# Input, memory, gains and convolution taps handed over as columns in a three-layer transformer kernel

## Chip, cores and metric

The kernel runs on one core of one Trainium2 chip. The metric is the device time of one execution in microseconds (us); lower is better.

## What is computed

One sequence of 256 positions, width 1024, goes through two layers of one kind and one of another, all in fp32. Cut to what matters here:

```python
def rms_norm(x, g):
    y = x * rsqrt(mean(x * x, axis=-1, keepdims=True) + EPS)
    return y * g

for layer in range(2):
    if layer == 1: shared_kv = shared_moba_kv(h, positions, kv_norm_g, w_kv, k_norm_g)
    h = h + 0.5 * swiglu(rms_norm(h, ffn1_norm_g[layer]), ...)       # width 2816
    u = rms_norm(h, mix_norm_g[layer]) @ w_in
    primary = conformer_conv(...) if layer == 0 else moba_attention(...)
    mem_out = memory_attention(q_mem, rms_norm(mem, mem_norm_g[layer]), w_mem_kv[layer], ...)
    h = h + concat([primary, mem_out]) @ w_o[layer]
    h = h + 0.5 * swiglu(rms_norm(h, ffn2_norm_g[layer]), ...)
h = second_block(h, norm_pre, norm_post, w_in, ..., conv_qk, ...)    # attention, mLSTM
```

`conformer_conv` is a depthwise convolution of 31 taps over 768 channels with a bias, then a layer norm and silu. `mem` has 256 rows of 1024; keys and values of each layer are `rms_norm(mem, g) @ w_mem_kv`. The second block has a depthwise convolution of 4 taps (`conv_qk`).

## The kernel before

Activations are held as columns: 128 partitions by 8 chunks by 256 positions (`hT`). Each product is made in single fast passes of a split number: an operand is rounded to a high part (`xh`, `whi`, by ScalarE) and a rest (`xl`, `wlo`, by VectorE), and three of the four products are summed. The weights are cut by `weight_plan` (L126) into 403 slots of up to 128x1024 numbers (512 KB). SyncE loads slot j into one of seven raw buffers once the rest of slot j-7 is made (L2892). `use(slot)` on ScalarE and VectorE (L1297, L1900) splits the slots up to slot+4 into five buffers each, and before that runs what `side(slot)` has for this slot. TensorE takes the slots in order; a slot of a feed-forward product is four groups, each of two 512-wide products with the high weights and two 256-wide with the rests (`two_blocks`, L541). `side` (L512) puts small products between slots. So each engine's order is written out by hand, and semaphores named in `signals` (L329) tie them.

**Start (L687, L1390, L2028, L2869).** SyncE loads a row of gains, then x in two tiles of 128 rows (512 KB each), then weight slots. TensorE turns the gain row and the 16 blocks of x; ScalarE and VectorE copy them from PSUM into `hT`. ScalarE rounds `hT` times gain into `xh` (`prep`), VectorE makes `xl`, and both split the first slots. Then come the squares for the first norm: ScalarE squares the four pairs of chunks (128x512), VectorE adds them into `acc` (`squares`, L1976), and `norm_sums` (L649) sums them over the partitions by four small products at slots 3, 75, 101, 169, 237, 269 and 337 (`NORM`, L35).

**Gains (L681, L1408, L1910).** The other seven gain rows are loaded by SyncE at slot 4 into `grow`, turned by TensorE at slot 6 and copied by VectorE. `mem_gain_load` waits on ScalarE for that copy, then loads the memory's gain row to all partitions over the same buffer.

**Memory (L1410, L1416, L2004, L665).** ScalarE loads `mem` as rows at slot 5 after six small loads, squares it at slot 12, and POOL makes the rows' norm factors. VectorE multiplies rows, factor and gain (`mem_row`: slots 16, 33, 37). TensorE turns the 16 blocks of each layer in groups of eight at slots 18, 20, 36 and 40 (`turn`), and ScalarE and VectorE split them (`turned`). The products are at slots 28 (`MKV0`) and 86 (`MKV1`); ScalarE reads them out by `mem_rows` (L1552).

**Taps (L760, L2120, L2847, L2881, L1051).** SyncE loads the 31 taps, bias and layer norm rows, TensorE turns them in six products at slot 46, VectorE copies them twice, SyncE writes one copy to DRAM and reads it back by fours. The four-tap rows are turned in eight products at slot 337.

## Time and profile before

| | us |
|---|---|
| median of 3 runs | 1241.22 |
| lowest, highest | 1240.76, 1243.17 |
| profiled execution, its own time | 1241.3 |
| its span, first to last instruction | 1239.7 |
| TensorE busy in the span | 1216.3 (98%) |
| VectorE, ScalarE, POOL busy | 882.0, 681.1, 60.6 |
| TensorE's mean granted clock | 0.996 |

The page gives busy time per engine and the costliest groups of instructions. The timeline lists instructions in order of time, where x14 says that fourteen were merged; the brackets tell how long the engine stood idle before and what released it. SPq and ACTq are DMA issues of SyncE and ScalarE. PE is TensorE, DVE VectorE, ACT ScalarE.

### The profile page before, as it was taken

The numbers are of one execution on the slowest core, as the hardware profiler recorded it, in microseconds if no ns is written. First come the engines' busy times: TensorE is split into PE (matmuls) and PEld (weight loads), VectorE is DVE, ScalarE is ACT, GpSimd is POOL, SyncE is SP. The second block draws the span as 40 slices with busy tenths as digits, with TensorE's granted clock in tenths as the row PEclk, the third lists the DMA queues.
The fourth block names the chain that finished last, engine by engine and source line by source line (L and its number), as shares of the span: only waits on it lengthen the run. The fifth ranks groups of instructions, "written<-read, shape, count | busy, mean of one in ns | idle before, by whom it ended". The sixth has DMA issues, their size and how long they took to land.

```text
span 1239.7 us, 18893 instructions
## 1 busy us (share of the span) xinstructions
PE 1216.3 (98%) x7518; PEld 1066.9 (86%) x7518; DVE 882.0 (71%) x1256; ACT 681.1 (55%) x1032; POOL 60.6 (5%) x89
## 2 busy tenths in 40 slices
PE   7999999989999999999999999999999999999998
PEld 6888888967888888888888888988888899888996
DVE  6686856875787775777775677577776666666875
ACT  5655544533666554555554456656555545556463
POOL 4000100100010000000000122000000000000000
PEclk9999999989999999999999999999999999999999
DMA  8766566671466655666655556047665566556450
GB/s 273 229 206 195 169 186 199 208 185 42 154 201 189 189 177 186 196 188 187 192 179 180 162 175 191 26 128 215 186 199 173 177 189 184 169 139 181 141 171 34
DMA packets 205654, 215.46 MB, mean 174 GB/s; under 512 B 9809, under 2 KB 192593, under 8 KB 205567
## 3 DMA queue, kind: packets, MB, share of 16 engines
q1 hardware_dynamic: 202998, 210.76, 56.5%
q10 hardware_dynamic: 2568, 3.50, 0.8%
q8 instruction: 60, 0.98, 0.3%
q14 instruction: 28, 0.22, 0.1%
HBM read 212.19 MB, written 2.03 MB: 173 GB/s over the span
## 4 chain that ended last, share of the span: by engine, by line
PE 90%; DVE 4%; ACT 4%; issue 2%; DMA 0%; ACTq 0%; POOL 0%; SPq 0%
PE psum L505 88%; DVE wlo L1896 1%; ACT whi L1294 1%; PE psum L671 0%; PE psum L953 0%; DMA xn<-in_x 0%; ACT qn L1598 0%; PE psum L699 0%; DVE x L1988 0%; ACT qT L1659 0%; ACTq L1409 0%; ACT L1735 0%; DVE small L2487 0%; ACT zob L1735 0%; ACT pb L1780 0%
## 5 line engine op out<-in xcount | busy, mean ns | idle before, releaser
L505 PE MATMUL psum<-x,whi 128*128 128x512 f32 (+1 forms) x2288 | 636.2, 365 | 3.8 <-ACT whi L1294 2.4
L1896 DVE TENSOR_TENSOR wlo<-raw,whi 128x1024 fp32r<-128x1024 f32 (+2 forms) x403 | 474.1, 1189 | 184.3 <-ACT whi L1294 181.3
L1294 ACT CAST whi<-raw 128x1024 fp32r<-128x1024 f32 (+2 forms) x403 | 406.0, 1022 | 163.2 <-PE psum L505 150.6
L505 PEld LDWEIGHTS psum<-x,wlo 128*128 128x128 f32 x1960 | 370.1, 189 | 74.3 <-DVE wlo L1896 1.8
L505 PE MATMUL psum<-x,wlo 128*128 128x256 f32 x1960 | 414.5, 279 | 0.7 <-DVE wlo L1896 0.7
L505 PEld LDWEIGHTS psum<-x,whi 128*128 128x128 f32 x2288 | 351.6, 190 | 5.8 <-ACT whi L1294 2.8
L505 PE MATMUL psum<-g,whi 128*128 128x512 f32 x704 | 220.1, 394 | 0.0
L505 PEld LDWEIGHTS psum<-g,wlo 128*128 128x128 f32 x704 | 132.2, 188 | 30.5
L505 PE MATMUL psum<-whi,x 128*128 128x512 f32 (+1 forms) x512 | 141.2, 376 | 0.1
L505 PE MATMUL psum<-g,wlo 128*128 128x256 f32 x704 | 139.2, 279 | 0.0
L505 PEld LDWEIGHTS psum<-g,whi 128*128 128x128 f32 x704 | 106.5, 188 | 0.0
L505 PEld LDWEIGHTS psum<-whi,x 128*128 128x128 f32 x512 | 90.0, 190 | 16.1 <-ACT zob L1707 0.3
L505 PE MATMUL psum<-wlo,x 128*128 128x512 f32 (+1 forms) x256 | 86.7, 374 | 0.0
L1341 ACT COPY pr<-psum 128x512 f32<-128x512 f32 x44 | 25.8, 586 | 66.3 <-PE psum L505 66.2
L1341 ACT COPY gr<-psum 128x512 f32<-128x512 f32 x44 | 25.8, 586 | 60.7 <-PE psum L505 60.5
L1970 DVE TENSOR_TENSOR pr<-psum,pr 128x512 f32<-128x512 f32 x44 | 30.4, 690 | 35.5 <-ACT pr L1341 35.5
L505 PEld LDWEIGHTS psum<-wlo,x 128*128 128x128 f32 x256 | 46.3, 190 | 8.6
L1371 ACT ACTIVATE x<-hT,gcol 128x256 fp32r<-128x256 f32 x64 | 28.5, 500 | 45.5 <-DVE hT L2105 29.1
L1970 DVE TENSOR_TENSOR gr<-psum,gr 128x512 f32<-128x512 f32 x44 | 30.3, 690 | 31.3 <-ACT gr L1341 31.2
L1988 DVE SCALAR_TENSOR_TENSOR x<-hT,gcol,x 128x256 fp32r<-128x256 f32 x64 | 28.8, 497 | 18.2 <-ACT x L1371 18.2
L1430 ACT ACTIVATE gr<-gr 128x512 f32<-128x512 f32 x44 | 27.7, 633 | 21.5 <-DVE gr L2054 21.5
L1439 ACT CAST g<-pr 128x512 fp32r<-128x512 f32 x44 | 27.4, 623 | 19.3 <-DVE pr L2062 19.3
(322 smaller groups left out, 851.5 us busy)
## 6 DMA issues: line engine op xcount, KB each, us to landing
raw<-in_ffn_w_gate SPq DMA_DIRECT2D x88, 512.0 KB, 4.4
raw<-in_ffn_w_up SPq DMA_DIRECT2D x88, 512.0 KB, 4.2
raw<-in_ffn_w_down SPq DMA_DIRECT2D x80, 512.0 KB, 3.9
raw<-in_w_in SPq DMA_DIRECT2D x52, 512.0 KB, 3.8
raw<-in_w_o SPq DMA_DIRECT2D x16, 512.0 KB, 4.6
raw<-in_a_w_in SPq DMA_DIRECT2D x14, 512.0 KB, 4.7
raw<-in_w_kv SPq DMA_DIRECT2D x16, 384.0 KB, 3.1
raw<-in_w_mem_kv SPq DMA_DIRECT2D x8, 512.0 KB, 3.9
```

Source lines behind the costliest of these rows:

```text
L505: return pe.matmul(o, l, r, start=start, stop=stop, skip_group_check=True)
L1294: act.copy(held(B.whi[:, i % SPLIT, :], *n), held(B.raw[:, i % RAW, :], *n)).then_inc(*s.hi.now(i))
L1341: act.copy(out, psum[:, b:b + 2, S:2 * S]).then_inc(*s.half.now(key))
L1371: act.activation(x[:, c, :], hT[:, c, :], ACT.Copy, scale=gcol[:, c, gi:gi + 1]).then_inc(*s.x_hi.now((gen, c)))
L1430: act.activation(r, r, ACT.Silu).then_inc(*s.silu.now((f, p)))
L1439: act.copy(F.gh[:, 2 * p:2 * p + 2, :], in_pairs(F.pr[:, p % 2, :])).then_inc(*s.g_hi.now((f, p)))
L1896: dve.tensor_tensor(held(B.wlo[:, i % SPLIT, :], *n), held(B.raw[:, i % RAW, :], *n), held(B.whi[:, i % SPLIT, :], *n).bitcast(F32), ALU.s ...
L1970: dve.tensor_tensor(out, psum[:, b:b + 2, 0:S], out, ALU.add).then_inc(*s.sum.now(key))
L1988: dve.scalar_tensor_tensor(out=xl[x][:, c, :], in0=hT[:, c, :], scalar=gcol[:, c, gi:gi + 1], in1=xh[x][:, c, :].bitcast(F32), op0=ALU.mul ...
```

## The change

The host lays out six arrays besides the weights: x and mem as columns, all ten gains as columns, the convolution taps with bias and layer norm rows as columns and a second time by fours, and the four taps as columns. The turning on TensorE and the copies behind it are gone. TensorE turns the identity eleven times at the start instead, into a bank that nobody reads. x comes in three pieces of 2, 2 and 4 chunks, the last behind two weight slots, and slot 0 is split in two halves; slot 2 is split before the squares. ScalarE issues the gains' load, and applies one silu first. The memory is loaded twice, as rows for the squares and as columns; ScalarE and VectorE split column chunk c times gain at slots 14 to 22 and 36 to 44, and `mem_rows` multiplies by the row's norm factor on reading out. VectorE adds the two halves of `acc` once more, and `norm_sums` has two products instead of four. `gcol` has ten columns, `mem` lies as 128 x 8 x 256, and `rows`, `tapp` and the DRAM tensor `tap_mem` are gone.

```diff
-    B.gcol = sb("gcol", [128, 8, 8])
+    B.gcol = sb("gcol", [128, 8, 10])
...
-    B.mem = sb("memt", [128, 2, D], F32, mm)
-    B.gn = sb("gnm", [128, D], F32, mm)
-    B.grow = B.gn[0:8, :]
-    B.xg0 = B.mkv2[:].rearrange("p l t n -> p l (t n)")
-    B.xg1 = [B.xg0[:, 1, :], flat(B.htmp[:])]
-    st0 = ExitStack()
-    B.xn = sb("xn", [128, 2, D], F32, st0)
-    st0.close()
+    B.mem = sb("memt", [128, 8, S], F32, mm)
+
+    B.memr = B.mkv2[:].rearrange("p l t n -> p l (t n)")
...
+        ready = {0: s.lo0.at("half"), 2: s.lo.at(0)} if slot == 0 else {0: s.lo.at(slot)}
+        pe.wait_ge(*(s.hi.at(slot) if slot else s.hi0.at("half")))
         for i, kc in enumerate(ks):
             k = kc % 4
+            if slot == 0 and i == 2:
+                pe.wait_ge(*s.hi.at(0))
...
-        pe.wait_ge(*s.acc.at((n, 3)))
-        for tt in range(2):
-            for j in range(2):
-                t = mm(bank[b][:, 4 * tt:4 * tt + 4], B.acc[:, j * 256 + tt * 128:j * 256 + (tt + 1) * 128],
-                       ones[:, 0:4], j == 0, j == 1)
+        pe.wait_ge(*s.acc.at((n, 4)))
+        for tt in range(2):
+            t = mm(bank[b][:, 4 * tt:4 * tt + 4], B.acc[:, tt * 128:(tt + 1) * 128], ones[:, 0:4], True, True)
...
     def start():
+
         pe.wait_ge(*s.consts.at("ident"))
-        pe.wait_ge(*s.ld_g0.at("all"))
-        for c in range(8):
-            t = pe.transpose(bank[4][:, c:c + 1], B.grow[0:1, c * 128:(c + 1) * 128], ident[0:1, 0:1])
-        t.then_inc(*s.pe_set.now("g0"))
-        for p in range(4):
-            for tt in range(2):
-                if p == 0:
-                    pe.wait_ge(*s.ld_x[tt].at("all"))
-                for j in range(2):
-                    c = 2 * p + j
-                    t = pe.transpose(bank[p][:, j * 256 + tt * 128:j * 256 + (tt + 1) * 128],
-                                     B.xn[:, tt, c * 128:(c + 1) * 128], ident[:])
-            t.then_inc(*s.pe_set.now(f"x{p}"))
+        for i in range(11):
+            pe.transpose(bank[7][:, i % 4 * 128:(i % 4 + 1) * 128], ident[:], ident[:])
...
-        if slot == 6:
-            mem_gain_load()
         if slot == 12:
             mem_squares()
-        if slot == 18:
-            turned("mem0", 0, 8, xh[1], 0, [4, 5])
-        if slot == 20:
-            turned("mem0", 1, 8, xh[1], 0, [6, 7])
+        if 14 <= slot < 22:
+            mem_cols(0, slot - 14)
         if slot == MKV0 + 4:
             mem_rows(0, MKV0 + 3, 4)
         if slot in (34, 36):
             mem_key_squares(0, (slot - 34) // 2, B.sqb)
-        if slot in (36, 40):
-            tt = (slot - 36) // 4
-            turned("mem1", tt, 8, xh[1], 0, [[4, 5], [6, 7]][tt])
+        if 36 <= slot < 44:
+            mem_cols(1, slot - 36)
...
     def start():
-        for p in (1, 3):
-            act.wait_ge(*s.pe_set.at(f"x{p}"))
-            act.copy(flat(hT[:, 2 * p:2 * p + 2, :]), bank[p]).then_inc(*s.h_act.now(p))
-        act.wait_ge(*s.gcol.at("g0"))
+        act.dma_start(gcol[:], A["gain_cols"]).then_inc(*s.ld_gcol.now("all"))
+        act.wait_ge(*s.consts.at("ones"))
+        act.activation(small[0:1, 319:320], B.ones[0:1, 0:1], ACT.Silu)
+        act.wait_ge(*s.ld_gcol.at("all"))
         for p in range(4):
-            if p % 2 == 0:
-                act.wait_ge(*s.h.at((0, p)))
-            elif p == 1:
-                act.wait_ge(*s.h_act.at(3))
+            if p < 3:
+                act.wait_ge(*s.ld_x[p].at("all"))
             prep(0, p, [("f0", 0, xh[0])])
-            if p < 2:
-                split_to(p)
+            if p == 1:
+                act.wait_ge(*s.w[0].at(0))
+                act.copy(B.whi[:, 0, 0:512], B.raw[:, 0, 0:512]).then_inc(*s.hi0.now("half"))
+                act.copy(B.whi[:, 0, 512:1024], B.raw[:, 0, 512:1024]).then_inc(*s.hi.now(0))
+                splits[0] += 1
+                split_to(1)
+        split_to(2)
         for p in range(4):
             squares(0, p)
 
@@ -1407,17 +1345,23 @@
         for i, g in enumerate((A["mem_q_norm_g"][0], A["mem_k_norm_g"][0], A["mem_k_norm_g"][1], A["k_norm_g"],
                                A["b_q_norm_g"][0], A["mem_q_norm_g"][1])):
             act.dma_start(B.hg[:, i, :], rows128(g)).then_inc(*s.ld_hg.now(i))
-        act.dma_start(B.mem[:], A["mem"][0].rearrange("(t p) d -> p t d", p=128)).then_inc(*s.ld_mem.now("all"))
-
-    def mem_gain_load():
-        act.wait_ge(*s.gcol.at("all"))
-        act.dma_start(B.gn[:], rows128(A["mem_norm_g"][0])).then_inc(*s.ld_gn0.now("all"))
+        act.dma_start(B.memr, A["mem"][0].rearrange("(t p) d -> p t d", p=128)).then_inc(*s.ld_memr.now("all"))
+        act.dma_start(B.mem[:], A["mem_cols"]).then_inc(*s.ld_mem.now("all"))
 
     def mem_squares():
-        act.wait_ge(*s.ld_mem.at("all"))
-        for tt in range(2):
-            act.activation(B.xg0[:, tt, :], B.mem[:, tt, :], ACT.Square,
-                           accum_out=small[:, 24 + 2 * tt:25 + 2 * tt]).then_inc(*s.msq.now(tt))
+        act.wait_ge(*s.ld_memr.at("all"))
+        for tt in range(2):
+            act.activation(B.memr[:, tt, :], B.memr[:, tt, :], ACT.Square,
+                           accum_out=small[:, 312 + 2 * tt:313 + 2 * tt]).then_inc(*s.msq.now(tt))
+
+    def mem_cols(l, c):
+
+        if c == 0 and l == 0:
+            act.wait_ge(*s.ld_mem.at("all"))
+        elif c == 0:
+            act.wait_ge(*s.used.at(MKV0 + 3))
+        act.activation(xh[1][:, c, :], B.mem[:, c, :], ACT.Copy, scale=gcol[:, c, 8 + l:9 + l]).then_inc(
+            *s.x_hi.now((f"mem{l}", c)))
...
     def mem_rows(l, slot, b):
         act.wait_ge(*s.used.at(slot))
         for tt in range(2):
-            act.copy(B.mkv[l][:, tt, :], bank[b + tt]).then_inc(*s.kv.now((l, tt)))
+            act.wait_ge(*s.rstd.at(("mem", tt)))
+            act.activation(B.mkv[l][:, tt, :], bank[b + tt], ACT.Copy, scale=small[:, 313 + 2 * tt:314 + 2 * tt]).then_inc(
+                *s.kv.now((l, tt)))
...
+        if 15 <= slot < 23:
+            mem_cols(0, slot - 15)
...
+        if 37 <= slot < 45:
+            mem_cols(1, slot - 37)
...
+        if p == 3:
+            dve.wait_ge(*s.acc.at((v, 3)))
+            dve.tensor_tensor(B.acc[:, 0:S], B.acc[:, 0:S], B.acc[:, S:2 * S], ALU.add).then_inc(*s.acc.now((v, 4)))
...
-    def mem_row(l, tt, out):
-        dve.wait_ge(*s.rstd.at(("mem", tt)))
-        dve.scalar_tensor_tensor(out=out, in0=B.mem[:, tt, :], scalar=small[:, 25 + 2 * tt:26 + 2 * tt],
-                                 in1=B.gn[:], op0=ALU.mult, op1=ALU.mult).then_inc(*s.mrow.now((l, tt)))
+    def mem_cols(l, c):
+        dve.wait_ge(*s.x_hi.at((f"mem{l}", c)))
+        dve.scalar_tensor_tensor(out=xl[1][:, c, :], in0=B.mem[:, c, :], scalar=gcol[:, c, 8 + l:9 + l],
+                                 in1=xh[1][:, c, :].bitcast(F32), op0=ALU.mult, op1=ALU.subtract).then_inc(
+            *s.x_lo.now((f"mem{l}", c)))
...
-        dve.wait_ge(*s.pe_set.at("g0"))
-        dve.tensor_copy(gcol[:, :, 0], bank[4][:, 0:8]).then_inc(*s.gcol.now("g0"))
-        for p in (0, 2):
-            dve.wait_ge(*s.pe_set.at(f"x{p}"))
-            dve.tensor_copy(flat(hT[:, 2 * p:2 * p + 2, :]), bank[p]).then_inc(*s.h.now((0, p)))
         for p in range(4):
             prep(0, p, [("f0", 0, 0)])
-            if p < 2:
-                split_to(p)
+            if p == 1:
+                dve.wait_ge(*s.hi0.at("half"))
+                dve.tensor_tensor(B.wlo[:, 0, 0:512], B.raw[:, 0, 0:512], B.whi[:, 0, 0:512].bitcast(F32),
+                                  ALU.subtract).then_inc(*s.lo0.now("half"))
+                dve.wait_ge(*s.hi.at(0))
+                dve.tensor_tensor(B.wlo[:, 0, 512:1024], B.raw[:, 0, 512:1024], B.whi[:, 0, 512:1024].bitcast(F32),
+                                  ALU.subtract).then_inc(*s.lo.now(0))
+                splits[0] += 1
+                split_to(1)
+        split_to(2)
...
-    pool.wait_ge(*s.mrow.at((1, 1)))
-    pool.memset(MA.rows[0:32, :], 0.0).then_inc(*s.fills.now("rows"))
...
-        sp.wait_ge(*s.fills.at("rows"))
-        sp.dma_start(MA.rows[0:31, :], A["a_dw_kernel"][0].rearrange("k a c -> k (a c)")).then_inc(*s.ld_rows.now(0))
-        for i, nm in enumerate(("a_dw_bias", "a_ln_g", "a_ln_b")):
-            sp.dma_start(MA.rows[32 + i:33 + i, :], A[nm]).then_inc(*s.ld_rows.now(1 + i))
+        sp.wait_ge(*s.x_lo.at(("mem1", 7)))
+        sp.dma_start(MA.taps[:], A["conv_taps"]).then_inc(*s.ld_taps.now("all"))
+        sp.dma_start(MA.tap4[:], A["conv_taps_by_four"]).then_inc(*s.ld_tap4.now("all"))
...
+    def input_cols(i):
+        q = slice((0, 2, 4)[i], (2, 4, 8)[i])
+        sp.dma_start(B.hT[:, q, :], A["x_cols"][:, q, :]).then_inc(*s.ld_x[i].now("all"))
+
+    input_cols(0)
+    input_cols(1)
     for j, (w, k0, nk, c0, n) in enumerate(weight_plan(A)):
-        if j == 4:
-            for i in range(1, 8):
-                sp.dma_start(B.grow[i:i + 1, :], gains[i]).then_inc(*s.ld_gr.now(i))
-        if j == 20 + AHEAD + RAW:
-            sp.wait_ge(*s.pe_T.at(("mem0", 1, 1)))
-            sp.dma_start(B.gn[:], rows128(A["mem_norm_g"][1])).then_inc(*s.ld_gn1.now("all"))
-        if j == 50:
+        if j == 2:
+            input_cols(2)
+        if j == 56:
             conv_loads()
-        if j == 59:
-            sp.wait_ge(*s.taps.at("by_four"))
-            sp.dma_start(B.tap_mem, MA.tapp[:].rearrange("p j c m -> p (j c m)")).then_inc(*s.st_taps.now("all"))
-        if j == 61:
-            sp.wait_ge(*s.st_taps.at("all"))
-            for q in range(4):
-                sp.dma_start(MA.tap4[32 * q:32 * q + 32].rearrange("p g c m -> p g (c m)"),
-                             B.tap_mem.rearrange("(g c) n -> c g n", c=32)[:, :, 48 * q:48 * q + 48]).then_inc(
-                    *s.ld_tap4.now(q))
...
+def in_cols(rows):
+
+    a = np.asarray(rows)
+    return a.reshape(a.shape[0], -1, 128).transpose(2, 1, 0)
+
+
+def laid_out(inputs):
+
+    def get(name):
+        return np.asarray(inputs[name])
+
+    gains = [get("ffn1_norm_g")[0], get("mix_norm_g")[0], get("ffn2_norm_g")[0], get("kv_norm_g"), get("ffn1_norm_g")[1],
+             get("mix_norm_g")[1], get("ffn2_norm_g")[1], get("norm_pre_2")[0], get("mem_norm_g")[0], get("mem_norm_g")[1]]
+    kernel31 = get("a_dw_kernel")[0, :, 0, :]
+    none = np.zeros_like(kernel31[:1])
+    taps = in_cols(np.concatenate([kernel31, none, get("a_dw_bias"), get("a_ln_g"), get("a_ln_b")]))
+
+    by_four = taps[:, :, 0:32].reshape(4, 32, 6, 8, 4).transpose(4, 1, 0, 2, 3).reshape(128, 4, 6, 8)
+    return {"x_cols": in_cols(get("x")[0]), "mem_cols": in_cols(get("mem")[0]), "gain_cols": in_cols(np.stack(gains)),
+            "conv_taps": taps, "conv_taps_by_four": by_four, "short_taps": in_cols(get("conv_qk_2")[0])}
```

Left out are the signals' names, the removed `other_gains`, `conv_taps` and `short_taps`, and waits that name the new loads (on ScalarE and VectorE before the first use of the taps). SyncE's two tap loads stand at slot 56 instead of 50 to 61. The four-tap columns are loaded by ScalarE where it loaded the rows before (L1739).

## Rows read from the trace of the kernel before

**Rows 1.** The page's part 1 and part 5: TensorE, and VectorE's weight rests.
```profile
PE 1216.3 (98%) x7518; PEld 1066.9 (86%) x7518; DVE 882.0 (71%) x1256; ACT 681.1 (55%) x1032; POOL 60.6 (5%) x89
...
L1896 DVE TENSOR_TENSOR wlo<-raw,whi 128x1024 fp32r<-128x1024 f32 (+2 forms) x403 | 474.1, 1189 | 184.3 <-ACT whi L1294 181.3
```

**Rows 2.** Waits of PE over the span: total us, times, longest us.
```profile
PE psum L505 <- issue: 4.5, 1, 4.5
...
PE psum L505 <- DVE pr L1970: 0.9, 1, 0.9
```

**Rows 3.** Timeline of the first 28 us: start us, us, engine, line, operation.
```profile
0.79 0.34 SPq L2869 DMA_DIRECT2D gnm<-in_ffn_norm_g  x1
...
1.18 0.83 SPq L2871 DMA_DIRECT2D xn<-in_x  x2
...
6.12 3.25 PE L699 MATMUL psum<-ident,xn 128*128 128x128 f32 x14 [0.63 <-DMA xn<-in_x]
...
9.89 0.91 ACT L1371 ACTIVATE x<-hT,gcol 128x256 fp32r<-128x256 f32 x2
...
10.44 0.95 DVE L1988 SCALAR_TENSOR_TENSOR x<-hT,gcol,x 128x256 fp32r<-128x256 f32 x2 [1.19 <-ACT x L1371]
10.70 1.03 ACT L1294 CAST whi<-raw 128x1024 fp32r<-128x1024 f32 x1
...
11.76 1.69 DVE L1896 TENSOR_TENSOR wlo<-raw,whi 128x1024 fp32r<-128x1024 f32 x1 [0.38 <-ACT whi L1294]
...
11.78 1.22 PE L505 MATMUL psum<-x,whi 128*128 128x512 f32 x2 [2.41 <-ACT whi L1294]
...
15.39 1.05 PE L505 MATMUL psum<-x,whi 128*128 128x512 f32 x2
...
16.67 1.03 PE L505 MATMUL psum<-x,whi 128*128 128x512 f32 x2
...
27.45 0.63 PE L505 MATMUL psum<-x,whi 128*128 128x512 f32 x2
```

**Rows 4.** Landing of the first weight slice, issued at 2.06 us.
```profile
DMA to landing us min/median/max: 5.5/5.5/5.5
```

**Rows 5.** Stretches: us, busy per engine, granted clock, DMA share, GB/s.
```profile
10.00:12.00 2.00, 0.22 (x1) 0.22 (x2) 1.19 (x3) 2.00 (x4) 1.77 (x3) 1.00 1.10 350
...
69.70:81.00 11.30, 11.30 (x70) 9.98 (x69) 10.68 (x15) 7.71 (x12) 0.00 (x0) 1.00 0.76 225
...
268.00:272.00 4.00, 3.33 (x32) 1.84 (x36) 3.14 (x8) 1.02 (x4) 0.00 (x0) 0.50 1.10 342
```

**Rows 6.** Timeline of PE around gain, memory and square sum products.
```profile
33.24 0.40 PE L505 MATMUL psum<-x,wlo 128*128 128x256 f32 x2
...
34.73 0.39 PE L505 MATMUL psum<-x,wlo 128*128 128x256 f32 x2
...
35.42 0.40 PE L505 MATMUL psum<-x,wlo 128*128 128x256 f32 x2
...
68.70 0.40 PE L505 MATMUL psum<-x,wlo 128*128 128x256 f32 x2
...
70.27 0.40 PE L505 MATMUL psum<-x,wlo 128*128 128x256 f32 x2
...
344.13 0.39 PE L505 MATMUL psum<-x,wlo 128*128 128x256 f32 x2
...
345.71 0.40 PE L505 MATMUL psum<-x,wlo 128*128 128x256 f32 x2
```

**Rows 7.** Timeline of DVE: the last square addition before the third norm.
```profile
342.42 0.69 DVE L1982 TENSOR_TENSOR acc<-acc,sqb 128x512 f32<-128x512 f32 x1
```

**Rows 8.** Timeline of ACT: the memory load's issue, the wait for the gains.
```profile
34.15 0.46 ACTq L1410 DMA_DIRECT2D memt<-in_mem  x1
...
39.54 1.05 ACT L1294 CAST whi<-raw 128x1024 fp32r<-128x1024 f32 x1 [3.31 <-DVE gcol L1910]
```

**Rows 9.** Landing of the memory load, issued at 34.15 us.
```profile
DMA to landing us min/median/max: 10.0/10.0/10.0
```

More of the change, by code:

```diff
@@ L452, in signals @@
     s.lo = sig("w_lo", range(SLOTS))
-    s.gcol = sig("gain_cols", ["g0", "all"])
-    s.h = sig("h", [(0, 0), (0, 2)] + [(v, p) for v in range(1, 7) for p in P4])
-    s.acc = sig("square_sums", [(v, p) for v in range(7) for p in range(1, 4)])
+    s.lo0 = sig("first_lo", ["half"])
+    s.h = sig("h", [(v, p) for v in range(1, 7) for p in P4])
+    s.acc = sig("square_sums", [(v, p) for v in range(7) for p in range(1, 5)])
     s.nv = sig("norm_var", range(7))
@@ L460, in signals @@
     s.g_lo = sig("ffn_lo", ffn_pairs)
-    s.mrow = sig("mem_rows", [(l, t) for l in T2 for t in T2])
-    s.taps = sig("taps", ["all", "by_four"])
     s.w4 = sig("conv_weights", CONV_PE)
@@ L732, in ffn @@
                 pe.wait_ge(*s.kT0.at((0, 1)))
-            if f == 0 and p == 1:
-                pe.wait_ge(*s.taps.at("by_four"))
             if f == 1 and p == 1:
@@ L754, in down @@
                     pe.wait_ge(*s.g_lo.at((f, kc // 2)))
-                t = two_blocks(b, h[:, k, :], l[:, k, :], F.g[:, kc], kc == 0, kc == 21, i if k == 0 else None)
+                t = two_blocks(b, h[:, k, :], l[:, k, :], F.g[:, kc], kc == 0, kc == 21, s.lo.at(i) if k == 0 else None)
             t.then_inc(*s.used.now(i))
             i += 1
-    def conv_taps():
-        pe.wait_ge(*s.ld_rows.at(3))
-        for c in range(6):
-            t = pe.transpose(bank[6][:, c * 35:(c + 1) * 35], MA.rows[:, c * 128:(c + 1) * 128], ident[0:35, 0:35])
-        t.then_inc(*s.pe_a.now("taps"))
     def query_rows():
@@ L1048, in att_turn @@
         t.then_inc(*s.pe_T.now(("o1", tt, i)))
-    def short_taps():
-        pe.wait_ge(*s.ld_crow.at("all"))
-        pe.wait_ge(*s.h.at((6, 3)))
-        for c in range(8):
-            t = pe.transpose(bank[5][:, c * 4:(c + 1) * 4], MC.crow[:, c * 128:(c + 1) * 128], ident[0:4, 0:4])
-        t.then_inc(*s.pe_c.now("ctap"))
     def gate_cols():
@@ L1947, in side @@
             rotary()
-        if slot == QK2 + 3:
-            dve.wait_ge(*s.pe_c.at("ctap"))
-            dve.tensor_copy(flat(MC.ctap[:]), bank[5][:, 0:32]).then_inc(*s.ctap.now("all"))
     def norm_cols(n):
```

118 lines of the change are left out of this document (31 added, 87 removed).

## The prediction

> **What bounds the kernel now.** I read the page first. TensorE is busy for 1216.3 of 1239.7 us [rows 1], so what is taken from TensorE's own list comes off the time, and what is taken from another engine does so only where TensorE waits for it. Next, TensorE's waits: behind the start there are few, 4.5 us in the convolution stage, which this change leaves in place, and 0.9 us for the second up product's sum (DVE pr) [rows 2]. Then the timeline of the start [rows 3]. The reader is to see three things there. The first product of a weight runs only at 11.78. Its groups (two high, two rest products) then come every 1.28 us (15.39 to 16.67) where a later one needs 0.70 (34.73 to 35.42, [rows 6]). And slot 3 is over only at 27.45. All that is ahead of this point can be shortened by an earlier start, and what stands behind it is a nearly gapless row.
>
> The sum is made against the profiled execution's own 1241.3 us (span 1239.7 and 1.6 around it), which stands 0.1 above the median of 1241.22.
>
> **Start.** Loads first. SyncE's first x load moves from 1.18 to the place of the gain row at 0.79, 0.39 earlier [rows 3]. Before, all of x (1 MB) has landed by 6.12 and slot 0 by 2.06 + 5.5 = 7.56 [rows 4]. Transfers run at 350 GB/s [rows 5], 1.5 us for 512 KB. Now 512 KB stand ahead of slot 0 instead of 1 MB: x's first piece lands at about 3.5, the second at 4.25, slot 0 at 7.56 - 0.39 - 1.5, with 0.1 for the gains' columns 5.8, slot 1 at 7.3, the rest of x at 8.8, slot 2 at 10.3. ScalarE scales four chunks at 0.46 each (0.91 for two) [rows 3]: done at 5.4. It waits for slot 0 and rounds half of it in 0.55 (1.03 for the whole): TensorE starts at 6.35. VectorE's half rests are ready at 7.05 and 7.75 (0.69 for a 128x512 operation, [rows 7]).
>
> TensorE's pace: before, four groups went by at 1.28 or slower, then came 0.70. I take the same four: 6.35 + 4 x 1.28 = 11.45. Slots 1 and 2 are eight groups at 0.70: 17.05. The norm's sums, halved, are 0.44 (below), slot 3 another 2.8: 20.3. Does VectorE keep up? Rests of slot 1 from 8.4 to 9.6 (mean 1.19, [rows 1]), four chunks of x at 0.475 [rows 3] to 11.5, slot 2 from 11.7 to 12.9 (13.4 at the 1.69 of [rows 3]), three square additions and the fold to about 16, slot 3 to 17.3. TensorE wants them at 14.6, 17.05 and 18.0: just in time. Slot 3 ends 27.45 - 20.3 = 7.15 earlier, of which 0.44 belongs to the norm below: **6.7**. Bounds: if the slow pace lasts 3 us longer (1.5) and loads or VectorE come 1 us later, about 4; if TensorE is fast from 6.35, VectorE's rests of slot 3 at 17.3 hold the end at about 19.5, and the gain is 7.5. With slot 0 landing 0.7 earlier than I work out it is 8.2.
>
> The clock. The granted clock's column has no lower value this early, but the groups' pace does show the lower level of 1.2 GHz. Fourteen turns of x took 3.25 us, 0.23 each [rows 3], where eight later ones cost 0.11 each [rows 6], and they did not lift it: the groups behind them were slow. The eleven turns of the identity are the same kind of work, from about 1.6 to 4.1, and then TensorE idles until 6.35. Hence four slow groups in my sum.
>
> The Trainium skill ("TensorE: Matmul & The Clock Gate", Part 4, PE-mode transpose) says that transposes do not count as busy work for the clock. By that rule the eleven turns buy nothing, which is the sum above. The trace agrees as far as it goes: x's turns lifted nothing. Without the rule the sum would be 0.8 less.
>
> **TensorE's list behind the start.** A pair of rest products normally follows the last by 0.70 [rows 6].
> - Memory turns: from 68.70 to 70.27 are 1.57 [rows 6], so eight turns cost 0.87. There are four such groups: **3.5**.
> - Seven gain rows, eight small turns: 33.24 to 34.73, 1.49 - 0.70 = 0.79 [rows 6]. The four taps are eight turns of this kind (0.79), the 31 taps six (0.59): together **2.2**.
> - Norm sums: 344.13 to 345.71 is 1.58, so 0.88 for four products, of which two go: 0.44, seven times **3.1**.
>
> **The wait of 0.9.** Early in the first feed-forward ScalarE stands 3.31 us at 39.54 for the turned gains [rows 8], then loads a function table at its first silu. Both go (the silu's set is loaded at the start, under the loads). One load issue comes in its place, at 0.46 [rows 8]. ScalarE comes out over 4 us earlier, and this wait goes: **0.9**. What is late next there is nothing that TensorE asks for. Bounds: 0 to 0.9.
>
> **What is added.** The fold of `acc` is one 128x256 addition on VectorE per norm; the nearest row is 0.475 for a 128x256 operation [rows 3]. The last addition before the third norm is over at 343.11 [rows 7], TensorE asks at 344.36, so it does not wait. But the fold delays the next rests and the gate's sum, which TensorE needs about 0.5 us after it is made, and TensorE itself arrives 0.44 earlier. I take **-0.3** over all norms, bounds 0 and 7 x 0.48 = -3.4. The column copies of the memory are 16 of 0.46 to 0.5 on ScalarE and VectorE. VectorE is busy for 10.68 of 11.30 us in such a stretch [rows 5], but in those eight slots it loses four subtractions of 0.69 and two wide products of about 1.2 (5.2) and gains 8 x 0.475 = 3.8: no cost; their cover is TensorE's gapless row, and without it they would be 0.475 apiece. Scaling on reading out costs what the copy did. SyncE loses eighteen small issues, gains three, and loses its waits for turned memory and taps, POOL a fill: nobody waits for these. SyncE's new wait at slot 56 is for a rest made at slot 44, before the rest of slot 49 that this load needs anyway.
>
> **Sum:** 6.7 + 3.5 + 2.2 + 3.1 + 0.9 - 0.3 = 16.1. 1241.3 - 16.1 = **1225.2 us**.
>
> **Rivals.**
> - *The turns do lift the clock.* Against: x's turns did not. For: they come in one dense run, where x's waited for loads. VectorE becomes the limit at slot 3: 0.8 less, 1224.4.
> - *The convolution stage changes level differently.* There the granted clock is 0.50 around 268 to 272 [rows 5], behind the wait of 4.5. The next copy of this stage comes at another moment. Without the low stretches up to 4 us are won, 1221; with one more, 3 are lost, 1228.
> - *The start is worth half.* Loads arrive later or POOL's constants slow VectorE (1.69 instead of 1.19): 3 us less, 1228.2.
> - *VectorE is already the bound in the dense stretches of the first feed-forward.* Then the memory turns' 3.5 and a fold's -3.4 at worst fall away: 1229 to 1232. Against: TensorE shows no wait there.
> - *Slower than before: the memory's columns come too late.* The place is ScalarE's copy at slot 14, in front of all later roundings. One MB needed 10.0 us from its issue among the weights [rows 9], so two need about 20. Issued at about 27, they are down at 47; slot 13 begins at 45.5, and ScalarE is four slots (11 us) ahead of TensorE. So TensorE waits only past 57, and all 16 us are eaten if the columns land after 73. That takes a second load over three times as slow as the first. Hardly.
> - *It does not do what it says*: the gaps are filled by other waits of the same length, no change.
>
> **Chances.** Forecast 0.53, clock lifted 0.12, convolution stage 0.13, half a start 0.11, VectorE 0.07, slower 0.02, no change 0.02. A measurement of this kernel tells 0.2%, 2.5 us, from no change. All cases but the last two are beyond that: faster 0.96, same 0.02, slower 0.02. The range of 1219.5 to 1230.5 takes in the bounds of the start (4 to 8.2), the fold's middle and the convolution stage's levels on both sides.
>
> **What would show it.** Right: the first product of a weight near 6.35, four slow groups, slot 3's end near 20.3; no turned memory; 0.44 less at each norm; no wait for DVE pr. The start's step is wrong if that end is past 23; the wait step if ScalarE's first silu is not reached earlier; the fold's if TensorE shows waits for acc or gr behind the norms. The forecast as a whole is wrong if a new wait of over 3 us stands in TensorE's list.

## The result and the profile after

The changed kernel takes 1224.06 us (median of 4, 1222.81 to 1224.45), beside 1241.05 for the kernel before on the same chip. The ratio is 0.9858, with a 95% interval of 0.9841 to 0.9875: 17.0 us less, where 16.1 were forecast. The profiled execution took 1224.19 (span 1222.9), 17.1 less than that of before. That the sum came out does not mean that its terms did, so I went through it stretch by stretch.

The page of the changed kernel, parts 1 and 5, answers to [rows 1]. Of the 6.4 us that TensorE stands idle ahead of its high products (`whi`), 4.5 now stand ahead of the first of them.
```profile
PE 1201.9 (98%) x7423; PEld 1054.7 (86%) x7423; DVE 878.8 (72%) x1261; ACT 681.9 (56%) x1039; POOL 63.5 (5%) x88
...
L490 PE MATMUL psum<-x,whi 128*128 128x512 f32 (+1 forms) x2288 | 627.7, 362 | 6.4 <-ACT whi L1336 4.5
```

Waits of PE over the span of the changed kernel (total us, times, longest us), to be read beside [rows 2].
```profile
PE psum L490 <- ACT whi L1336: 4.5, 1, 4.5
PE psum L490 <- issue: 3.1, 1, 3.1
...
PE psum L657 <- POOL ident L2665: 1.6, 1, 1.6
PE psum L490 <- DVE gr L1899: 1.1, 1, 1.1
```
The wait for DVE pr (0.9) is gone, as forecast. The convolution stage's wait is 3.1 instead of 4.5. New is 1.1 for DVE gr. (`pr` and `gr` are the running sums of the up and the gate product, which VectorE makes.)

Timeline of the start of the changed kernel (start us, us, engine, line, operation, wait before it), beside [rows 3].
```profile
1.57 2.61 PE L657 MATMUL psum<-ident 128*128 128x128 f32 x11 [1.57 <-POOL ident L2665]
...
5.08 0.91 ACT L1306 ACTIVATE x<-hT,gcol 128x256 fp32r<-128x256 f32 x2 [2.35 <-DMA gcol<-in_gain_cols]
...
5.62 0.88 DVE L1920 SCALAR_TENSOR_TENSOR x<-hT,gcol,x 128x256 fp32r<-128x256 f32 x2 [5.62 <-ACT x L1306]
...
7.71 4.82 POOL L2682 TENSOR_SCALAR alib<-kTm 128x256 bf16<-128x256 f32 x4
8.02 0.62 ACT L1336 CAST whi<-raw 128x512 fp32r<-128x512 f32 x1 [0.78 <-DMA raw<-in_ffn_w_gate]
...
8.69 1.22 PE L490 MATMUL psum<-x,whi 128*128 128x512 f32 x2 [4.52 <-ACT whi L1336]
...
11.74 3.48 DVE L1920 SCALAR_TENSOR_TENSOR x<-hT,gcol,x 128x256 fp32r<-128x256 f32 x4
...
12.68 1.07 POOL L2683 TENSOR_SCALAR_AFFINE_SELECT alib<-alib 128x1024 bf16<-128x1024 bf16 x1
...
12.80 1.05 PE L490 MATMUL psum<-x,whi 128*128 128x512 f32 x2
...
13.89 1.06 POOL L2685 TENSOR_SCALAR_AFFINE_SELECT alib<-alib 128x1024 bf16<-128x1024 bf16 x1
...
14.08 0.80 PE L490 MATMUL psum<-x,whi 128*128 128x512 f32 x2
...
14.95 0.62 PE L490 MATMUL psum<-x,whi 128*128 128x512 f32 x2
...
18.95 4.62 DVE L1844 TENSOR_TENSOR wlo<-raw,whi 128x1024 fp32r<-128x1024 f32 x4
...
24.23 0.72 PE L490 MATMUL psum<-x,whi 128*128 128x512 f32 x2 [1.07 <-DVE gr L1899]
```
The first product runs at 8.69, not 6.35. Four groups are slow (8.69 to 14.08), as forecast. Slot 4's first product, which stood at 27.45, stands at 24.23 behind a wait of 1.07: 3.2 us are won where 7.15 were expected. That is also the prediction's own sign for a wrong start ("if that end is past 23"). The four x chunks on VectorE cost 0.87 each on average (3.48 for four) instead of 0.475, and they were not slow alike. The view of 13.9 to 15.1 us gives the last two of them:
```profile
12.68 2.55 DVE L1920 SCALAR_TENSOR_TENSOR x<-hT,gcol,x 128x256 fp32r<-128x256 f32 x2
```
The first two, from 11.74 on, followed each other by 0.47, these two took 1.27 each, and these ran beside GpSimd's two affine selects over 128x1024 (12.68 and 13.89). GpSimd's multiplies for `alib` did no such harm: the two chunks at 5.62 ran beside them (3.34 to 7.21) and took 0.44 each.

Why is the first product late? Here are the loads issued between 1.5 and 2 us (operation, KB each, us to landing), changed kernel:
```profile
raw<-in_ffn_w_gate SPq DMA_DIRECT2D x1, 512.0 KB, 6.3
```
Slot 0 lands at 1.70 + 6.3 = 8.0, not 5.8. And the stretches 3:4 and 4:6 (us, busy per engine, granted clock, DMA share, GB/s), first in the kernel before:
```profile
3.00:4.00 1.00, 0.38 (x4) 0.29 (x3) 0.17 (x1) 0.00 (x0) 0.91 (x2) 1.00 0.94 369
4.00:6.00 2.00, 0.69 (x2) 0.29 (x2) 0.00 (x0) 0.00 (x0) 1.83 (x3) 1.00 0.99 371
```
and in the changed one:
```profile
3.00:4.00 1.00, 1.00 (x6) 0.78 (x4) 0.00 (x0) 0.00 (x0) 0.91 (x2) 1.00 0.62 165
4.00:6.00 2.00, 0.18 (x1) 0.00 (x0) 0.38 (x1) 0.91 (x2) 1.83 (x3) 1.00 0.91 277
```
The same queues move less than half as much at 3 to 4 us, and 277 instead of 371 GB/s in the next two. My 350 GB/s was the rate of weight slots at 10 to 12 us.

**Where the rest came from.** I compared the same products in both timelines. What the changed kernel gained, us, by stretch (span, 16.8 in all):

| stretch | gained | the forecast's steps in it | left over |
|---|---|---|---|
| start to slot 4 | 3.2 | 7.15 | -3.9 |
| slot 4 to norm 1 | 6.4 | turns 3.5 + 0.79 + 0.59, wait 0.9 = 5.8 | +0.6 |
| norm 1 to the convolution | 2.25 | 0.44 | +1.8 |
| to norm 2 | 0.45 | 0 | +0.45 |
| norm 2 to 3 | 0.85 | 0.44 | +0.4 |
| norm 3 to 4 | 2.05 | 0.44 | +1.6 |
| norm 4 to 5 | -1.55 | 0.44 | -2.0 |
| norm 5 to 6 | 1.0 | 0.44 | +0.5 |
| norm 6 to the end | 2.2 | 0.79 + 0.44 | +0.9 |

So TensorE's list came as worked out, the start 3.9 short, and 4 us came back from the last column. Of these 1.4 are the convolution's shorter wait (4.5 to 3.1). The others stand in stretches where TensorE never waits, or waits as long as before to within 0.3. Rows ten and more groups apart show what they are. A group is two high products and two rest products. First and last high products of gapless runs in the kernel before: 18 groups on x, 43 on g of the first feed-forward, 42 on g of the third:
```profile
76.95 0.62 PE L505 MATMUL psum<-x,whi 128*128 128x512 f32 x2
...
89.49 0.62 PE L505 MATMUL psum<-x,whi 128*128 128x512 f32 x2
...
179.82 0.62 PE L505 MATMUL psum<-g,whi 128*128 128x512 f32 x2
...
209.64 0.62 PE L505 MATMUL psum<-g,whi 128*128 128x512 f32 x2
...
660.13 0.63 PE L505 MATMUL psum<-g,whi 128*128 128x512 f32 x2
...
689.67 0.63 PE L505 MATMUL psum<-g,whi 128*128 128x512 f32 x2
```
and in the changed kernel, 42 on x, 42 on g of the first, 42 on g of the third:
```profile
60.21 0.62 PE L490 MATMUL psum<-x,whi 128*128 128x512 f32 x2
...
89.19 0.62 PE L490 MATMUL psum<-x,whi 128*128 128x512 f32 x2
...
149.86 0.63 PE L490 MATMUL psum<-g,whi 128*128 128x512 f32 x2
...
179.12 0.63 PE L490 MATMUL psum<-g,whi 128*128 128x512 f32 x2
...
659.99 0.62 PE L490 MATMUL psum<-g,whi 128*128 128x512 f32 x2
...
689.25 0.62 PE L490 MATMUL psum<-g,whi 128*128 128x512 f32 x2
```
A group takes 12.54/18 = 0.6967 on x before, 28.98/42 = 0.690 after. On g it went from 0.6935 to 0.6967, on the third g from 0.7033 to 0.6967. The instructions are the same. What differs is where the buffers lie: `gcol` has ten columns instead of eight, and all that is laid behind it has moved by 64 bytes a partition. The third g has moved by 96, since an unused buffer of 16 bytes (`even`), which the printed diff leaves out, stands ahead of it.

Most of the -2.0 between norms 4 and 5, 1.6, is the clock (experiment 4 lacks it there). Stretches of the changed kernel, columns as above:
```profile
759.00:763.00 4.00, 2.39 (x14) 2.14 (x15) 1.36 (x6) 3.80 (x17) 0.00 (x0) 0.87 0.43 150
763.00:767.00 4.00, 4.00 (x25) 3.81 (x24) 2.20 (x6) 2.35 (x9) 0.00 (x0) 0.70 0.00 0
```
The granted clock is 1.00 in the same place of the kernel before, though TensorE's wait of 2.1 for qn ahead of it is the same in both.

### The profile page after: what moved, and what is told of

It reads as the page before. It is cut to its first block, busy times and chain, and to the rows that moved or that the text cites. A ratio compares the mean times of both kernels' runs of the same rounds, so it can differ in the third digit from the quotient of the medians.

```text
span 1222.9 us, 18713 instructions
## 1 busy us (share of the span) xinstructions
PE 1201.9 (98%) x7423; PEld 1054.7 (86%) x7423; DVE 878.8 (72%) x1261; ACT 681.9 (56%) x1039; POOL 63.5 (5%) x88
## 4 chain that ended last, share of the span: by engine, by line
PE 85%; DVE 7%; ACT 5%; DMA 2%; issue 1%; SPq 0%; POOL 0%; ACTq 0%; DVEq 0%
PE psum L490 83%; DVE wlo L1844 3%; ACT whi L1234 2%; DVE hT L2048 1%; DMA raw<-in_ffn_w_up 1%; DMA conv_mem<-hc 1%; DMA h<-conv_mem 1%; PE psum L901 0%; ACT x L1306 0%; ACT qn L1546 0%; DVE acc L1911 0%; DVE x L1920 0%; ACT sqb L1296 0%; DVE qk L2405 0%; ACT qT L1607 0%
## 5 line engine op out<-in xcount | busy, mean ns | idle before, releaser
L490 PE MATMUL psum<-x,whi 128*128 128x512 f32 (+1 forms) x2288 | 627.7, 362 | 6.4 <-ACT whi L1336 4.5
```

The lines of the kernel that those rows point to most:

```text
L490: return pe.matmul(o, l, r, start=start, stop=stop, skip_group_check=True)
```

## The experiments

Each is timed against the kernel before on its own chip; medians of before lie between 1241.24 and 1242.02. Rows are from one execution of each. From one such execution to another with the same start, the landing of a load differs by some tenths of a microsecond, once by 0.8.

**1. Place of the buffers, kernel before.**
```diff
+    sb("pad64", [128, 16])
     B.gcol = sb("gcol", [128, 8, 8])
```


> The kernel before with 64 unused bytes per partition ahead of the gain columns, nothing else. This moves x and g to the addresses they have in the changed kernel (g of the third feed-forward keeps an offset of its own). Placement theory: a group on x (two high, two rest products) falls from 0.697 us to 0.690, one on g rises from 0.6935 to 0.697, and the time falls by 2 to 5 us to about 1237. Rival (the shorter groups come from what else the change removed, less traffic from the other engines): groups stay at 0.697 and 0.6935, the time stays at 1241 within 1 us.

1238.66 (1237.86 to 1240.29, 11 runs), ratio 0.9976, 0.9967 to 0.9985. Unused bytes alone give 2.7 us. Groups on x take 0.690, on g 0.6967, on the third g 0.7026. The profiled execution hides a part: slot 0 took 6.3 us to land instead of 5.5, with nothing changed in the loads, and the first norm's products stand at 24.90 instead of 23.78.

**2. The other way round, changed kernel.**
```diff
     B.gcol = sb("gcol", [128, 8, 10])
+    B.maskb = sb("maskb", [128, 128], BF16)
+    B.ident4 = sb("ident4", [128, 32])
+    B.mhalf = sb("mhalf", [128, 16])
+    B.hg = sb("hg", [128, 6, 64])
...
     B.ident = sb("ident", [128, 128])
...
-    B.maskb = sb("maskb", [128, 128], BF16)
-    B.ident4 = sb("ident4", [128, 32])
...
-    B.mhalf = sb("mhalf", [128, 16])
-    B.hg = sb("hg", [128, 6, 64])
```


> The changed kernel with four small buffers allocated ahead of x instead of behind it, so that x lies at the old address modulo 2048 bytes and g where the changed kernel has it. Placement theory: groups on x go back to 0.697 us, groups on g stay at 0.697, and the time rises by about 5 us (some 820 groups of 6.4 ns) to 1229. Rival (less traffic): groups on x stay at 0.690 and the time at 1224.

1228.35 (1227.0 to 1230.5), ratio 0.9895, 0.9882 to 0.9909: 4.3 us worse than the changed kernel, groups on x back at 0.6967, g unmoved. So the place of x alone is worth about 4. The span of the profiled execution is only 2.8 above: it has no low-clock stretch around the convolution.

**3. Norm sums.** Four products again, and no fold.
```diff
-        pe.wait_ge(*s.acc.at((n, 4)))
+        pe.wait_ge(*s.acc.at((n, 3)))
         for tt in range(2):
-            t = mm(..., B.acc[:, tt * 128:(tt + 1) * 128], ones[:, 0:4], True, True)
+            for j in range(2):
+                t = mm(..., B.acc[:, j * 256 + tt * 128:...], ones[:, 0:4], j == 0, j == 1)
```


> The changed kernel with the square sums as before: four small products per norm and no fold on VectorE. The prediction's step: 7 x 0.44 = 3.1 us more on TensorE, less 0.3 for the fold: 1226.9. If TensorE has slack at these places or the fold costs what it saves: 1224 within 1 us. The wait for the gate's sum at slot 4 should shrink by the fold's 0.3 to 0.45 us in any case.

1226.5 (1225.5 to 1227.29), ratio 0.9879, 0.9865 to 0.9892: +2.4. The second norm's products in the timeline of PE, in this kernel
```profile
215.88 0.95 PE L490 MATMUL psum<-ones,acc 128*128 128x4 f32 x8
```
and in the changed one
```profile
216.70 0.50 PE L490 MATMUL psum<-ones,acc 128*128 128x4 f32 x4
```
The difference is 0.45 a norm, 3.1 over seven. The wait for gr at slot 4 is 0.46 here and 1.07 there: with the fold VectorE is later, and TensorE, through with its sums 0.45 sooner, waits instead. So 0.6 is lost at the first norm, and 3.1 - 0.6 = 2.5 is near the +2.4. The rows carry this, not the total: the intervals of the two kernels overlap, and this execution lacks the low clock near 763 but has 3.4 us more of it near 290.

**4. Turned memory.** Eight identity turns at each of four slots of the changed kernel.
```diff
+        if slot in (18, 20, 36, 40):
+            for i in range(8):
+                pe.transpose(bank[6 + i // 4][...], ident[:], ident[:])
```


> The changed kernel with eight turns of the identity put back into TensorE's list at slots 18, 20, 36 and 40, read by nobody: only TensorE's time of the memory turns. The prediction's step: 4 x 0.87 = 3.5 us more, 1227.6. Rival (another engine sets the pace in these stretches, so turns are hidden): 1224 within 1 us.

1225.6 (1223.48 to 1226.79), ratio 0.987, 0.9856 to 0.9883: +1.5. The stretch itself, from slot 4 to norm 1, is 3.4 longer. Timeline of PE in this kernel:
```profile
23.96 0.72 PE L490 MATMUL psum<-x,whi 128*128 128x512 f32 x2 [1.40 <-DVE gr L1902]
...
219.85 0.50 PE L490 MATMUL psum<-ones,acc 128*128 128x4 f32 x4
```
195.9 us, where the changed kernel has 216.70 - 24.23 = 192.5. The step holds. The total alone would not show it, since the intervals overlap. Of the 3.4, 0.3 was won before slot 4, 0.2 came back around the convolution, and 1.6 came back because this execution lacks the low clock near 763: from norm 4 to norm 5 it takes 120.3, where the changed kernel takes 121.9.

**5. No turns of the identity.** The loop of eleven (L656) is taken out.

> The changed kernel without the eleven turns of the identity at the start. The prediction's step (turns of this kind don't lift the clock): the groups from the first product on come every 1.28 us as with them, four to five of them, the start is unchanged and the time 1224. Rival (they shorten the slow stretch): one to three more slow groups of 0.59 us each, 1224.6 to 1226.

1222.31 (1220.82 to 1224.03), ratio 0.9844, 0.9827 to 0.9861. The first groups stand at 8.53, 9.95, 11.23, 12.51 and 13.79: as slow as in the changed kernel, and the intervals overlap. In the executions of experiments 4 and 10, which have the turns, the pace rises about two groups sooner, so one execution doesn't prove that turns never shorten the slow row. But slot 4 starts at 24.03 here and at 23.96 and 23.92 there: they buy next to nothing.

**6. Full-precision products in their place.**
```diff
-        for i in range(11):
-            pe.transpose(bank[7][...], ident[:], ident[:])
+        for i in range(20):
+            mm(bank[7][...], ident[:], ident[:], True, True)
```


> The changed kernel with twenty true 128x128 fp32 products of the identity in place of the eleven turns, dense from 1.6 us to near the first weight product. If real products lift the clock, the first groups come every 0.69 us instead of 1.28. Theory (VectorE's rests of slots 2 and 3 and its gate sum, at 16.4, 20.1 and 24.2, set the start's end): slot 4 still starts near 24.2, the time stays within 0.5 us of 1224, and new waits for wlo show. Rival (TensorE sets it): 2.5 us less, 1221.5.

1221.74 (1219.76 to 1222.99), ratio 0.9834, 0.9813 to 0.9854. Groups now follow every 0.69 from 9.44 on. But TensorE runs into VectorE: waits of 1.17 for a rest and of 1.40 for gr, and slot 4 starts at 23.89, only 0.34 sooner, which is what the first product is sooner (8.36):
```profile
23.89 0.72 PE L490 MATMUL psum<-x,whi 128*128 128x512 f32 x2 [1.40 <-DVE gr L1899]
```
At the start VectorE sets the end, not the clock. The lower total doesn't tell against it: the intervals overlap, and this execution lacks the low clock near 763.

**7. GpSimd's constants behind norm 0.** `alib` and `ident4` are made later.
```diff
     constants()
...
     norm(0)
+    late_constants()
```


> The changed kernel with POOL's bias tables and the narrow identities (alib, ident4) made behind the first norm instead of ahead of it. Theory (POOL's work slows VectorE's rests of x from 0.48 to 0.87 us each): four rests take 1.9 instead of 3.5 us, the wait of 1.07 for the gate's sum at slot 4 goes, 1223. Rival (the slow rests have another cause): they stay at 0.87 and the time at 1224.

1223.99 (1222.13 to 1225.64), ratio 0.9857, 0.9839 to 0.9874: no gain. Yet the timeline shows the contention away (VectorE's four x chunks, then slot 4 on PE without a wait):
```profile
11.60 1.67 DVE L1920 SCALAR_TENSOR_TENSOR x<-hT,gcol,x 128x256 fp32r<-128x256 f32 x4
```
```profile
22.84 0.62 PE L490 MATMUL psum<-x,whi 128*128 128x512 f32 x2
```
The chunks take 1.67 instead of 3.48, slot 4 starts 1.4 sooner. Of this 0.57 is lost again by 41 us, in waits for gr (0.34 at 34.84) and pr (0.23 at 40.88), where the constants now stand beside VectorE, and the lead is 0.56 at norm 1. Then the convolution's wait is 3.5 instead of 3.1, and 0.2 is left there and at the end. Moving the contention is not removing it. The selects and the multiplies moved together here; that it was the selects is read from the rows above, and from experiment 8, where the four chunks ran beside multiplies alone and took 1.94.

**8. x in contiguous pieces.** The host hands x over as three arrays, so a piece is no longer cut out of rows of 8 KB.
```diff
-        sp.dma_start(B.hT[:, q, :], A["x_cols"][:, q, :])
+        sp.dma_start(B.hT[:, q, :], A[f"x_cols{i}"])
```


> The changed kernel with the three pieces of x each contiguous in DRAM instead of cut out of rows of 8 KB. The first piece lands 4.1 us after its issue and slot 0 at 8.0, where the prediction had 3.5 and 5.8. Theory A (pieces of rows are slow to read): x at about 3.7, slot 0 at about 6.5, first product at 7 instead of 8.7. Theory B (the queue starts slowly whatever it reads, or the gains' short rows hold it up): slot 0 stays near 8.0, first product near 8.7, time 1224.

ScalarE's first x in the timeline of this kernel, and the load of slot 0 (operation, KB each, us to landing):
```profile
3.90 1.70 ACT L1306 ACTIVATE x<-hT,gcol 128x256 fp32r<-128x256 f32 x4 [1.17 <-DMA gcol<-in_gain_cols]
```
```profile
raw<-in_ffn_w_gate SPq DMA_DIRECT2D x1, 512.0 KB, 5.0
```
Slot 0 lands 1.3 sooner, the first product runs at 7.41, and at 3 to 4 us the queues carry 362 GB/s instead of 165. For x's own pieces the cause is shown: they landed in 3.0, and in 3.4 in experiments 11 and 12, where cut pieces took 4.2 to 4.6. For slot 0 it is shown only in part: it landed at 6.7 here, but at 7.6 in experiments 11 and 12 with the same contiguous x, and at 7.7 to 7.9 in seven other executions with cut pieces. The time is 1225.4 all the same (1224.99 to 1225.93), ratio 0.9869, 0.9854 to 0.9884: slot 4 starts at 23.00 behind a wait for gr of 1.43 (here the selects stand beside the square additions, three of which take 3.81 instead of 2.29), and in the convolution stage a wait of 2.1 for a load appears where the changed kernel has 0.3, with a low-clock stretch of 6.8 us. Why that stage answers so to a start 1.2 us sooner is open.

**9. Gains' load behind slot 0.** SyncE issues it instead of ScalarE.

> The changed kernel with the load of gains and taps (rows of 320 bytes) issued by SP behind slot 0 instead of by ACT at 0.8 us. Theory A (slot 0 and the x columns come late because the many short rows of gains and taps share the queues with them): slot 0 lands 1 us or more sooner than 8.0, and if ACT has gains by about 6 all the same the first product stands at about 7.7; slot 4 at 24.23 all the same or 0.3 sooner, since VectorE sets it. Theory B (the x columns, 2 KB pieces cut out of 8 KB rows, are what is slow, and gains cost nothing): slot 0 lands at 8.0 within 0.3; gains now land last, at about 6.5 to 8.5, the x work of ACT begins that much later, and the first product stands at 9 to 10.5; slot 4 up to 1.5 later than 24.23. Time: A 1223 to 1224, B 1224 to 1225.7.

1224.56 (1223.47 to 1227.64), ratio 0.9874, 0.9857 to 0.989. Slot 0 lands at 1.70 + 5.9 = 7.6, 0.4 sooner than in the changed kernel and 0.1 sooner than in several executions with its loads, gains at 7.85, so the first product runs at 10.11 and slot 4 at 25.13. The short rows of the gains hold the others up by little.

**10. g moved too.** 576 unused bytes ahead of each feed-forward's g, 128 in the third.
```diff
     def ffn_space(f):
+        sb(f"gpad{f}", [128, 32 if f == 2 else 144], F32, c)
```


> The changed kernel with unused bytes ahead of the feed-forwards' own buffers (576 a partition, 128 for the third feed-forward), so that every g begins at 1344 bytes beyond a multiple of 2048, as x does in the changed kernel. Nothing else moves; the instructions are the same. Placement theory in its plain form (one rule by the moving operand's own address holds for x and for g): a group of four products on g takes 0.690 us as one on x does, not 0.697; there are about 350 such groups, so 2.2 to 2.5 us come off, 1221.7. Rival A (it is the place relative to another buffer, or there is no common rule, and 704 was only a lucky place for g): groups on g stay at 0.697 or go to 0.7033, and the time is 1224 or up to 1226.3. x groups stay at 0.690 in every case.

1221.35 (1220.91 to 1224.42), ratio 0.9845, 0.983 to 0.986: 2.7 below the changed kernel, with intervals that overlap. Of this 1.6 is the low clock near 763, which this execution lacks; the first g's gain is lost in part to a new wait of 0.34 for gr, the second and fourth feed-forward take 0.6 less each. Groups on g take 0.690 in three feed-forwards, but 0.6967 in the third (43 groups of the first, 42 of the third, timeline of PE):
```profile
149.98 0.62 PE L491 MATMUL psum<-g,whi 128*128 128x512 f32 x2
...
179.65 0.62 PE L491 MATMUL psum<-g,whi 128*128 128x512 f32 x2
...
660.21 0.62 PE L491 MATMUL psum<-g,whi 128*128 128x512 f32 x2
...
689.47 0.62 PE L491 MATMUL psum<-g,whi 128*128 128x512 f32 x2
```
My addresses were sums of the buffers' sizes. The third g lies behind small buffers, and I had not thought of their sizes being rounded up. Rounded to 32 bytes, which fits the pace of every g here but is printed nowhere, the 128 bytes took it to a multiple of 256 (not to the place of x), and from here on I go by the distance from a multiple of 256.

**11. All together**: contiguous x, late constants, sixteen full-precision products in place of the turns, 64 unused bytes ahead of every g.

> A version meant to beat both: the changed kernel with x in three contiguous pieces, the constants of GpSimd that the start doesn't need behind norm 0, sixteen full-precision identity products in place of the eleven turns, and 64 unused bytes ahead of every feed-forward's g, so that all x and g buffers begin 192 bytes beyond a multiple of 256. Theory of the start: x and slot 0 arrive as with contiguous pieces, the first product stands at 7.2 to 7.6, the groups follow every 0.69 us at once, and since GpSimd is quiet VectorE no longer stretches; slot 4 at 20.5 to 21.5 with no wait or a short one for gr. Theory of placement (the distance from a multiple of 256 decides, whichever buffer it is): groups on g take 0.690 in all four feed-forwards, the third among them, which 128 bytes left at 0.697. Sum: 1224.06 - 3.0 (start) - 2.4 (352 groups by 0.0067) = 1218.7. Rival: VectorE runs late one or two slots further on, as it did with GpSimd's constants moved alone, and the start gives 1.5: 1220.2. Rival to placement: g with 64 bytes stays at 0.697 and only the 576 of the run before it had an effect; then 1221.

1221.1 (1219.02 to 1221.4), ratio 0.9832, 0.9818 to 0.9847. That is 20.9 us less than before, and some 3 less than the changed one, whose interval it just touches. All four g take 0.690, the third among them, as the expectation said. The start gave less than expected (timeline of PE):
```profile
8.28 0.74 PE L491 MATMUL psum<-x,whi 128*128 128x512 f32 x2 [0.93 <-ACT whi L1337]
...
22.06 0.74 PE L491 MATMUL psum<-x,whi 128*128 128x512 f32 x2 [1.42 <-DVE gr L1900]
```
and the load of slot 0:
```profile
raw<-in_ffn_w_gate SPq DMA_DIRECT2D x1, 512.0 KB, 5.9
```
Slot 0 landed at 7.6 here, not at 6.7 as in experiment 8, and VectorE was late for gr again. 2.2 us are won at slot 4, and 0.58 of them is lost at 39.96 to a wait for pr. The total stands no clearly better than experiments 6 and 10, whose intervals overlap with this one.

**12. The weights' slots moved**, x and g at their place beyond a multiple of 256.
```diff
+    sb("pad64", [128, 16])
     B.raw = sb("raw", [128, RAW, SLOT])
...
+    sb("pad192", [128, 48])
     B.gcol = sb("gcol", [128, 8, 10])
```


> The same version with 64 unused bytes ahead of the weight slots and 192 ahead of the gains: raw, whi and wlo begin 192 bytes beyond a multiple of 256 instead of 128, and x and g move by 256 in all, so that they stand at 192 as before. Theory A (only the moving operand's own place beyond a multiple of 256 counts): all groups stay at 0.690 and the time is that of the version before it within 1 us. Theory B (its place relative to the weights' buffers counts; x and weights now have the same one, as they had before the change): groups go back to 0.697 and the time is 4 to 6.5 us longer. Theory C (the weights' own place adds its part): the groups take a value other than 0.690 with x unmoved, either way.

1227.87 (1225.43 to 1228.36), ratio 0.9885, 0.9869 to 0.9902: 6.8 us worse than experiment 11. The starts do not differ (first products at 8.29 and 8.28), but every group is back at 0.6967, here 43 on x:
```profile
59.76 0.63 PE L493 MATMUL psum<-x,whi 128*128 128x512 f32 x2
...
89.72 0.63 PE L493 MATMUL psum<-x,whi 128*128 128x512 f32 x2
```
Two of the low-clock stretches, near 290 and 763, stand in this execution and not in that of experiment 11, so the 6.8 is not all placement; the rows are. x has not moved against a multiple of 256, only what lies ahead of it has. So the rule that I had gone by, the operand's own distance from a multiple of 256, is wrong. Two rules are left that fit every group measured here. Either its distance from something ahead counts, perhaps from the weights' slots. Or its own place counts after all, but modulo 512: x and g moved by 256 bytes in this run. A run that moves the weights by 64 and x and g by 512 would tell them apart; none was made.

## Why the prediction was right, step by step

**The total** fell inside the range, 0.9 us beyond the sum on the gaining side. Two errors of about 4 us with opposite signs stand behind that, so that the number is as near as this is luck. What came at the start is the rival "the start is worth half" (0.11), for both of the reasons that it names; alone it would have given 1225.2 + 3.9 = 1229.

**Start: wrong, mis-sized.** It gave 3.2 with the norm's 0.44, not 7.15, less than my lower bound of 4 allowed. Three terms failed. *Slot 0 at 5.8*: it landed at 8.0, and the first product was 2.3 late. I gave x's pieces the 350 GB/s of weight slots, and at 3 to 6 us, with pieces of 2 KB cut out of 8 KB rows, the queues moved 165 to 277. That is 0.4 to 1.3 of it (experiments 8, 11 and 12). The other part is the 1.5 that I took off for half a megabyte less ahead of slot 0: with contiguous pieces it took 5.0 or 5.9 from its issue, against 5.5 with the whole megabyte ahead. Why is open. *VectorE just in time*: the chunks that I priced at 0.475 took 0.87 on average, two of them 1.27 beside GpSimd's selects (experiment 7), and the row of 1.69 that I had in hand spoke of it. *No wait behind the first norm*: 1.07 for gr, of which 0.6 goes with the fold (experiment 3). The four slow groups were right, the rival of a lifted clock was wrong (experiment 5), and its remark that VectorE would then be the limit was right (experiment 6). The Trainium skill ("TensorE: Matmul & The Clock Gate", Part 4, PE-mode transpose) says that a transpose doesn't count as busy in the way of other matmuls, so that the full clock doesn't come on. Experiments 5 and 6 agree: with and without turns the groups came every 1.28 (from 10.24 and from 9.95), with real products every 0.69.

**TensorE's list: right.** Memory turns 3.5 (3.4 in experiment 4). Norm sums 0.45 each where I had 0.44 (experiment 3). Gain and tap turns were not tried by themselves; the stretch that holds two of their three parts gave 6.4, where they, the memory and the wait make 5.8, and x's faster groups 1.0 more, g's slower ones 0.2 less.

**The wait of 0.9: right**, it is gone, and ScalarE's 3.31 us for the gains with it. **The fold**: -0.3 as a sum was too small by half, 0.6, all at the first norm, and by the prediction's own sign (a wait for gr behind a norm) this step is wrong in size. **The memory columns** came 11.8 us after their issue, far ahead of need, so the slower rival had no footing.

**The convolution stage**: its clock did come otherwise, near 257 to 261 and 291 to 295 with 3.4 us each instead of 6.8 (of which TensorE stood idle for 1.8) and 3.4, its wait fell by 1.4, and a new low stretch near 763 cost 1.6. These nearly cancel.

**What no step foresaw** is the place of the buffers: 2.7 us when moved in the kernel before, 4.3 when x was moved back in the changed one. The first also slows groups on g by 0.003 (some 260 of them, 0.8 us), and its profiled execution started 1.1 late and has a low-clock stretch near 773 that the kernel before lacks. How the rest of the difference divides is open. The diff did show it: `gcol` grew ahead of x. The term to add was "every buffer behind it moves by 64 bytes: some 830 groups on x and 350 on g by -0.0067 to +0.0067 each".

## What to carry to other kernels

When a buffer's size changes, look at the pace of a long gapless row of equal products before and after: a shift of 64 bytes was worth 3 to 4 us of 1240 here, as much as 32 turned blocks, and it can be had for nothing. Price a load by rows of loads with the same shape in memory, not by the rate that full-size slots reach. And where two engines will run closer together, ask which third engine works beside them just then: the gain ends at whichever is late next.
